# Shared-expert products in the octet of the kept pair, and one 4 MB transfer for a pair's gate and up matrices in the loops of a two-layer mixture-of-experts trunk

## The reference, cut to what matters

```python
def expert_block(args):
    rows, e = args
    xb = x_pad[rows]
    h = jax.nn.silu(xb @ w_gate[e]) * (xb @ w_up[e])
    return h @ w_down[e]
...
shared = (jax.nn.silu(xt @ ws_gate) * (xt @ ws_up)) @ ws_down
return (routed + shared).reshape(B, S, D)
```

## Time and profile before

| what | value |
|---|---|
| device time, median of 3 runs (lowest, highest) | 1185.26 us (1184.73, 1186.56) |
| span of the profiled execution, first to last instruction | 1183.3 us |
| what the runs have beyond that span | 1.4 to 3.3 us |
| PE busy | 97% of the span |
| DMA queue q1, share of 16 engines | 89.8% |
| granted TensorE clock, mean | 0.996 of full speed |

### The profile page before, as it was taken

One profiled execution on the slowest core, in us unless ns is written; L12 is line 12 of the kernel. 1 busy time (PEld: TensorE's weight loads), 2 busy tenths in 40 slices (PEclk: granted clock), 3 DMA queues, 4 the chain that ended last, 5 costly groups with the idle time before them and its releaser, 6 DMA issues.

```text
span 1183.3 us, 22174 instructions
## 1 busy us (share of the span) xinstructions
PE 1149.2 (97%) x8846; PEld 688.0 (58%) x8846; DVE 347.2 (29%) x912; ACT 300.0 (25%) x713; POOL 56.4 (5%) x100
## 2 busy tenths in 40 slices
PE   9999999999999999999999999999999899999995
PEld 6865755555555555554787647555555555555552
DVE  0445522222122212121523557221222222121224
ACT  1454222212122212121214533122221212221222
POOL 1431100000001000000011001000000010000000
PEclk9999999999999999999999999999999999999998
DMA  9945999999999999999990558999999999999995
GB/s 375 418 161 185 349 418 426 428 428 428 429 428 421 429 426 427 426 426 418 406 364 2 230 233 343 408 426 426 429 429 428 428 423 427 426 426 428 428 423 204
DMA packets 42732, 449.12 MB, mean 380 GB/s; under 512 B 4512, under 2 KB 4896, under 8 KB 14240
## 3 DMA queue, kind: packets, MB, share of 16 engines
q1 hardware_dynamic: 41648, 443.30, 89.8%
q10 hardware_dynamic: 1008, 4.73, 1.0%
HBM read 446.96 MB, written 1.05 MB: 379 GB/s over the span
## 4 chain that ended last, share of the span: by engine, by line
PE 85%; DMA 9%; DVE 3%; ACT 1%; issue 1%; DVEq 0%; SPq 0%; ACTq 0%
PE bank L1301 18%; PE bank L1328 17%; PE bank L1364 17%; PE bank L848 7%; PE bank L867 6%; PE bank L1372 5%; PE bank L906 4%; DMA store<-in_w_gate 4%; DMA store<-in_w_down 3%; DMA store<-in_w_in_b 2%; PE bank L1337 2%; PE bank L1196 1%; PE bank L1066 1%; PE bank L1077 1%; ACT work L1498 1%
## 5 line engine op out<-in xcount | busy, mean ns | idle before, releaser
L1301 PE MATMUL bank<-store,work 128*64 128x256 f32 x1984 | 227.8, 382 | 5.3 <-DMA store<-in_w_gate 5.3
L1328 PE MATMUL bank<-store,work 128*64 128x256 f32 x1952 | 225.3, 379 | 6.2 <-issue 6.2
L1364 PE MATMUL bank<-store,work 128*32 128x512 f32 x1888 | 218.4, 595 | 3.1 <-ACT work L1498 2.9
L1301 PEld LDWEIGHTS bank<-store,work 128*64 128x64 f32 x1984 | 137.0, 137 | 116.1 <-issue 41.1
L1328 PEld LDWEIGHTS bank<-store,work 128*64 128x64 f32 x1952 | 145.0, 137 | 75.7 <-issue 11.6
L2030 DVE SCALAR_TENSOR_TENSOR yhalf<-bank,gcol,yhalf 128x512 fp32r<-128x512 f32 x124 | 92.9, 751 | 219.1 <-ACT yhalf L1664 219.1
L2022 DVE TENSOR_TENSOR work<-work,bank 128x256 f32<-128x256 f32 x64 | 27.0, 422 | 346.9 <-PE bank L1328 346.9
L1664 ACT ACTIVATE yhalf<-bank,gcol 128x512 fp32r<-128x512 f32 x124 | 85.1, 688 | 172.1 <-PE bank L1364 172.1
L1364 PEld LDWEIGHTS bank<-store,work 128*32 128x32 f32 x1888 | 56.1, 109 | 122.4 <-issue 110.7
L1498 ACT ACTIVATE work<-bank 128x512 f32<-128x512 f32 (+4 forms) x177 | 78.0, 441 | 105.8 <-PE bank L848 47.3
L1498 ACT ACTIVATE back<-bank 128x128 fp32r<-128x128 bf16 x64 | 17.8, 278 | 282.0 <-PE bank L1269 282.0
(11 more groups left out here) (185 smaller groups left out, 822.7 us busy)
## 6 DMA issues: line engine op xcount, KB each, us to landing
store<-in_w_down SPq DMA_DIRECT2D x56, 2048.0 KB, 17.7
store<-in_w_gate SPq DMA_DIRECT2D x56, 2048.0 KB, 17.7
store<-in_w_up SPq DMA_DIRECT2D x52, 2048.0 KB, 19.2
store<-in_w_up SPq DMA_DIRECT2D x18, 1024.0 KB, 10.5
store<-in_w_gate SPq DMA_DIRECT2D x12, 1024.0 KB, 8.5
store<-in_w_in_b SPq DMA_DIRECT2D x3, 3072.0 KB, 22.4
store<-in_w_out SPq DMA_DIRECT2D x4, 2048.0 KB, 14.2
store<-in_w_down SPq DMA_DIRECT2D x6, 1024.0 KB, 11.7
```

The source lines that it names most:

```text
L1301: last = pe.matmul(gate_bank[slots_of(e), 0:HID], xg[:, k, slots_of(2 * j + e)], w[e][:, k, :], start=(k == 0), stop=(k == KT - 1))
L1328: last = pe.matmul(up_bank[slots_of(e), 0:HID], xg[:, k, slots_of(2 * j + e)], w[e][:, k, :], start=(k == 0), stop=(k == KT - 1))
L1364: last = pe.matmul(yb[half][rows_of(t, e), :], hT[b][:, f, slots_of(e, t)], w[e][:, f, half * 512:half * 512 + 512], start=(f == 0), stop= ...
```

## The change

Two things change in the expert part of both layers. First, a pair's gate and up matrices lie side by side in HBM (`w_gate_up`), in a row of 32 KB for each partition in place of 16 KB in each of two tensors, and in SP's two loops they come by one transfer of 4 MB, GU(n), which waits for `hidden` of pair n-2 and counts on the semaphore for which PE's gate product waits. Outside the loops the gate and up halves are still brought by separate transfers. Second, the shared products move from octet 6 to octet 4, the octet of the kept pair, and octets 5 and 6 become one loop on PE and ACT.

```diff
-RES_OCTET = RES_PAIR // OCT_PAIRS
-SHARED_OCTET = OCTETS - 2
+MID_OCTET = RES_PAIR // OCT_PAIRS
...
+    w_gate, w_up = w_gate_up[:, :, :, 0:2, :], w_gate_up[:, :, :, 2:4, :]
...
+            def reload_gate_up(l, units, i, b):
+
+                sp.wait_ge(sem(f"hidden_{l}"), units)
+                for k in (2 * b, 2 * b + 1):
+                    sp.sem_inc(sem(f"up_landed{k}_{l}"), 16)
+                src = w_gate_up[l, bass.ds(UNROLL * i + b, 1)].rearrange("a p m n -> (a p) (m n)")
+                sp.dma_start(matrices(matrix_at(b, 0, 0), 4), src).then_inc(sem(f"gate_landed{2 * b}_{l}"), 16)
...
                 with sp.Fori(2, RES_STEP - 1) as i:
-                    reload(l, UNROLL * i + 1, i + 1, 0)
+                    reload_gate_up(l, UNROLL * i + 1, i + 1, 0)
                     reload_down(l, UNROLL * i, i, 1)
-                    reload(l, UNROLL * i + 2, i + 1, 1)
+                    reload_gate_up(l, UNROLL * i + 2, i + 1, 1)
                     reload_down(l, UNROLL * i + 1, i + 1, 0)
...
                 with sp.Fori(RES_STEP + 1, STEPS - 2) as i:
-                    reload(l, UNROLL * i + 1, i + 1, 0)
+                    reload_gate_up(l, UNROLL * i + 1, i + 1, 0)
                     reload_down(l, UNROLL * i, i, 1)
-                    reload(l, UNROLL * i + 2, i + 1, 1)
+                    reload_gate_up(l, UNROLL * i + 2, i + 1, 1)
                     reload_down(l, UNROLL * i + 1, i + 1, 0)
...
                     for j in range(OCT_PAIRS):
-                        unit(r, RES_OCTET, j, kept=(j == 0), kept_before=(j == 1))
-                    with pe.Fori(RES_OCTET + 1, SHARED_OCTET) as o:
+                        unit(r, MID_OCTET, j, kept=(j == 0), kept_before=(j == 1), shared=j)
+                    with pe.Fori(MID_OCTET + 1, OCTETS - 1) as o:
                         for j in range(OCT_PAIRS):
                             unit(r, o, j)
-                    for j in range(OCT_PAIRS):
-                        unit(r, SHARED_OCTET, j, shared=j)
...
-                    with act.Fori(1, SHARED_OCTET) as o:
+                    with act.Fori(1, MID_OCTET) as o:
                         for j in range(OCT_PAIRS):
                             unit(r, o, j)
                     for j in range(OCT_PAIRS):
-                        unit(r, SHARED_OCTET, j, shared=j)
+                        unit(r, MID_OCTET, j, shared=j)
+                    with act.Fori(MID_OCTET + 1, OCTETS - 1) as o:
+                        for j in range(OCT_PAIRS):
+                            unit(r, o, j)
...
+    a["w_gate_up"] = np.concatenate([a["w_gate"], a["w_up"]], axis=3)
```

More of the change, by code:

```diff
@@ L79, in build_trunk @@
 def build_trunk(nc, x_in, xT_in, memT_in, w_in_a, sinks, w_in_b, lambda_qk, subln_g, w_mem_kv, w_out, ln_g, ln_b,
-                w_router, router_bias, w_gate, w_up, w_down, ws_gate, ws_up, ws_down, out):
+                w_router, router_bias, w_gate_up, w_down, ws_gate, ws_up, ws_down, out):
     slopes = [alibi_slopes(MIX_HEADS), alibi_slopes(DIFF_HEADS)]
     lam_init = 0.8 - 0.6 * math.exp(-0.3 * 1)
+    w_gate, w_up = w_gate_up[:, :, :, 0:2, :], w_gate_up[:, :, :, 2:4, :]
     jobs = [
@@ L1449, in _ @@
                         unit(r, 0, j, place=j)
-                    with pe.Fori(1, RES_OCTET) as o:
+                    with pe.Fori(1, MID_OCTET) as o:
                         for j in range(OCT_PAIRS):
@@ L2111, in laid_out @@
         a[name] = a[name].reshape(DEPTH, PAIRS, 2, P, MATRIX).transpose(0, 1, 3, 2, 4)
+    a["w_gate_up"] = np.concatenate([a["w_gate"], a["w_up"]], axis=3)
     return {name: np.ascontiguousarray(a[name]) for name in _INS}
 _INS = ["x", "xT", "memT", "w_in_a", "sinks", "w_in_b", "lambda_qk", "subln_g", "w_mem_kv", "w_out", "ln_g", "ln_b", "w_router",
-        "router_bias", "w_gate", "w_up", "w_down", "w_shared_gate", "w_shared_up", "w_shared_down"]
+        "router_bias", "w_gate_up", "w_down", "w_shared_gate", "w_shared_up", "w_shared_down"]
 def kernel(**inputs):
```

## The result

The changed kernel takes 1205.2 us, the median of 5 runs (1202.51 to 1205.86), against 1185.73 us for the kernel before beside it. The ratio is 1.016, with an interval of 1.0149 to 1.0171: 19.5 us slower. 1194.7 us was forecast, with a range up to 1199.0. The direction was right, the loss was double what I had worked out, and the time lies outside the range.

The account below looks back on a forecast made before the run. The prediction took the DMA stream up to D(30)'s landing as the bound: 4.4 us later in the first layer and 5.1 in the second, 9.5 in total on 1185.26, given as 1194.7 us; range 1189.5 to 1199.

Parts of the forecast that it names:

- What bounds the kernel: End of each layer: D(30)'s landing sets it; PE's time is free unless the DMA queue runs dry, which costs in full.
- a fixed tail: Behind D(30)'s landing in each layer: three PE products, the sums and the norm follow at once, unchanged in length.
- The ledger's rules: DMA queue behind the kept pair: landing is the later of previous landing and issue + 2.5 us, plus own time.
- The 4 MB transfers, own time: Merged loop transfers: 9.74 us each in place of 9.78, for 20 transfers a layer, saving 0.8 us.
- The 4 MB transfers, PE's wait: Pair 15: the gate product waits for the up matrices too, making PE 3.1 us later in both layers.
- a rival for PE's clock: Clock falls to half in one unit of each layer, 12 us of PE on top, over 1200; chance 0.02.
- The 4 MB transfers, their issue: SP's loops: gate half issued some 3.5 us later, free as long as the queue has over 2.5 us of work.
- The shared products: Octet 4: 7.2 us more PE time, in parts of 0.2, 1.9, 3.4 and 1.6, meeting the shortest backlog.
- The second layer: Same ledger moved by 598.2 us: D(30) lands at 1161.2 against 1156.1, 5.1 us later.
- The never-dry one: Rival at GU(22)'s issue: queue never dry, change faster, 1183.2 us, or 1180.8 with 0.1 a transfer; chance 0.06.
- the one with little start-up: Rival: with a queue nearly empty the next transfer's start is hidden; with no start-up 1189.8 us; chance 0.13.
- Dearer start-up: Rival: a transfer's start takes 4.1 us, from D(17)'s row, 2 x 1.6 more, 1198.0 us; chance 0.15.

Follow-up runs that it names:

- the late issue: Kernel before in joint layout, its looped gate and up as two 2 MB transfers, both issued behind the wait for `hidden`: 1188.44 us, ratio 1.0026.
- the second profile: The changed kernel run once more without edit, for another profile of it: 1205.39 us, with a span of 1203.7 for the profiled execution.

## Why the prediction went wrong, point by point

**What bounds the kernel** was right: D(30)'s landing sets the end of the first layer, PE's time is free until the queue runs dry, and most of the dry time is not made up (of 11.3 us at GU(23), 1.9 are). It was not wholly right at the end of the second layer, where I had a fixed tail behind that landing. In the profile of the changed kernel the last DMA of the chain is that for pair 27; its gate product ran with the clock low (5.36 us), and from there on the chain stays on PE:

```profile
1092.78 21.06 DMA store<-in_w_gate_up
1113.88 5.36 PE bank L1310 x32
...
1173.67 3.57 PE bank L1373 x32
```

The last of these rows reads D(30), and starts 1.1 us after its landing at 1172.5.

**The ledger's rules** are the step that failed. "A transfer lands at the later of (landing of the one before) and (issue + 2.5), plus its own time": the 2.5 us come from a truly empty queue. With a short backlog the start was 3.9 us at GU(22), 4.6 at the G(6) of the late issue, 5.0 at GU(6). What the windows show beside it is that the landing of the transfer before isn't the time when the engines run out: their traffic falls up to 3 us earlier. That this is the reason for the long start is argued, not shown. The earlier trace rows had told it: 3.7 us of backlog, and already 0.4 lost. I made it a rival at 0.15 and kept the lower value for the sum. Of the 5.0 us by which D(30) of the first layer is later than forecast, this rule makes 3.4: 1.4 directly at GU(22), and 2.0 at GU(6), which reach GU(22) through PE's lateness at pair 15. The other 1.6 are PE's clock.

**The 4 MB transfers, own time**: right, 9.7 us.

**The 4 MB transfers, PE's wait**: the mechanism was right, the size too small, 6.7 us at pair 15 of the first layer in place of 3.1. Of the missing 3.6, 2.0 are the stream's loss at GU(6), and 1.6 the clock: the up product starts 5.2 us behind the gate product and not 3.6. The kernels without these two waits (pairs 14 and 15 separate) show the weight of the term: 9 us of the total. I had a rival for PE's clock, but at 0.02, and with a wrong price: a whole unit at half clock, over 1200. It was 1.6 us at pair 15 of one layer. That the time came out over 1200 all the same is no merit of that rival; its mechanism made a small part of the loss.

**The 4 MB transfers, their issue**: "as long as the queue has over 2.5 us of work this is free" failed at the first looped pair, 1.4 us a layer in the experiment of the late issue, and once more behind the kept pair together with the shared products.

**The shared products** cost PE 7.2 us as worked out; they alone lose 3.7 us. By the ledger D(20), issued at 401.7 + 7.1 = 408.8, would be dry for 1.5 us, 3.0 in both layers.

**The second layer.** D(30) is issued at 1156.83 and lands 15.7 later by the same query, at 1172.5, against 1156.1 before: 16.4, of which 9.4 came with the first layer, so 7.0 for a forecast of 5.1. No clock fell at its pair 15 in this profile. GU(22) is issued at 1027.29, 0.7 us later than forecast if the first layer's 9.4 are allowed for, and lands after 13.5, a start of 3.8 in place of 2.5: together 2.0, the 1.9 that are missing. With the 1.1 of PE at the end, 9.4 + 7.0 + 1.1 are the 17.5 us by which the span grew. The median of the runs lies 2.7 us above the profiled execution; in the second profile, where the clock fell at pair 15 of both layers, the span is 2.9 longer.

**The rivals.** The never-dry one and the one with little start-up are excluded by 383 GB/s. Fixed cost per transfer is not given back by merging; 24 merged transfers give 2.0 us in all in one kernel (0.8 to 3.0), and in the other no more than the noise. "Dearer start-up" was the right rival, but it had been priced alone (1198.0), with GU(6) and the clock left out. My range was too narrow because I varied one term at a time, though each of them moves the same issue.

What stays open is how the start at a short backlog follows from the spread of the sixteen engines; it was 2.7 to 5.4 us in the changed kernel's profile, and 6.8 once with pairs 14 and 15 separate, with no order that I could find, and no experiment took it apart.

## What to carry to other kernels

In a kernel that streams weights through a full queue, look for the point with the shortest backlog, and charge every edit that delays PE or an issue ahead of it at that one point, all together: here 6.4 and 3.7 us alone became 19.5. Work that is free four pairs later (the shared products in octet 5) is not free there, and a merged transfer that is good where the queue is deep makes its reader wait for the last byte. Measure the backlog in engine activity (GB/s in windows of 1 to 2 us), not from landing to issue, which overstated it by up to 3 us here.

## What the runs showed of the hardware that I had not expected

The granted clock fell to the lower level, 0.50 in windows of 3.0 us, behind some waits of 2.3 us of PE between products that had kept it busy, and the gate product behind such a wait took 5.36 us in place of 3.67. Other waits of the same length (pair 15 in the kernel with the 4 MB transfers alone, 2.30 us, product 3.67) left it at 1.00. So did the two waits of 0.87 and 1.27 us of the kernel before.

A transfer issued when the one before it had 1.9 or 2.5 us to go took longer to start (4.6 us with 16 KB rows, 5.0 with 32 KB rows) than one issued into an empty queue (2.5). It was not so every time: D(17) of the changed kernel, issued when the one before it had 1.7 us to go, landed after 7.7, a start of 2.8.
